# Sixty-four chunks of tokens stand in the array and the state weights stream: a new injection for the bidirectional scan, with its states in token order

## The chip, the cores and the metric

The kernel runs on one core of one Trainium2 chip. The metric is the device time of one execution in microseconds (us); lower is better. Changes of under 0.2% can't be told from no change here.

## The reference, cut to what matters

Four layers of a diffusion backbone, batch 1, 256 latent tokens and 256 context tokens, width 1024, float32. Every layer is a token mixer and a SwiGLU channel mixer; each half ends in a join (residual, RMS norm, shift and scale from modulation vectors that come from `silu(c) @ mod_w + mod_b`, four layers times six vectors of 1024). The mixers are latent attention, Hyena, S5 and FNet, in this order. The change is in layer 2, the S5 mixer:

```python
# S5_GROUPS = 64 groups of 16 channels, S5_STATE = 64 complex states, two directions
def s5_scan(u, lam_bar, b_bar, h0, reverse):
    bu = jnp.einsum('bngc,gsc->bngs', u.astype(jnp.complex64), b_bar)
    a = jnp.broadcast_to(lam_bar, bu.shape)
    a_cum, xs = lax.associative_scan(_lin_rec, (a, bu), axis=1, reverse=reverse)
    ...
    return xs + a_cum * h0[:, None]      # x[t] = lam_bar * x[t-1] + b_bar u[t]
...
xs_ctx = s5_scan(u_ctx, ..., None, reverse)          # context first
xs_lat = s5_scan(u_lat, ..., h0, reverse)            # then the latents, from the context's last state
y_lat = y_lat + einsum(xs_lat, c_mat).real           # both directions are added
return a * jax.nn.sigmoid(b)   # a, b from gelu(y_lat) @ w_glu + b_glu
```

## The kernel before

Each engine runs its own list of instructions in program order, and semaphores tie the lists. The stages follow each other: setup, then for every layer mixer, join (`mid`), channel mixer (`Ffn`), join (`post`). Every matrix product but those of the S5 and FNet mixers and a few small ones is made of three products of rounded halves (lines 956 to 958).

**The S5 mixer** treats the sequence in chunks of STEP = 8 tokens, so that 256 latents are CH = 32 chunks and context and latents together are 64. Its weights are prepared during the channel mixers of layers 0 and 1 and wait in DRAM: `et` (what a chunk adds to the states), `m0` (what a chunk's tokens do to its own outputs), `f` (what the state before a chunk does to its outputs), and a table of powers.

1. The join before it writes the normed tokens into `h_split` (line 693), and 32 DMAs, 16 from SP's queue and 16 from GpSimd's (`tokens`, line 2253), bring them into `u`: for each of the 64 groups 128 partitions (8 tokens times 16 channels) and 64 chunks, latents first.
2. Injection (line 2475), in 16 rounds of four groups, NB = 16. The weights `et` stand in the array (128 columns, real and imaginary part apart) and the 64 chunks of `u` stream. A product of float32 shows as two passes in the trace, so 128 products are 256 passes. Partitions of the result are the states, 64 forward and 64 backward.
3. ScalarE takes each round's bank into `e` (line 2521) with three copies: context before latents for the forward direction, and reversed for the backward one. `e` holds for each group and part the place q in a block of 8 chunks first and the block b last, so a copy writes with a step of 32 bytes.
4. The scan runs on VectorE: `inside` (lines 2375 to 2378) goes from place to place for all 8 blocks at once, seven steps of four instructions, for groups 0 to 15, 16 to 31 and 32 to 63; `across` (2385 to 2388) goes from block to block on the last places, seven steps of four, for the first half (groups 0 to 31) and for the second; `carries` (2430 to 2433) adds to the other places what comes in from the block before, eight instructions of 896 elements. `carries` of the first half is on GpSimd, that of the second on VectorE.
5. TensorE meanwhile makes the products with `m0` (line 2489), and after ScalarE and VectorE have brought the states into `s2` (line 2521, 2451, 2452) those with `f` (line 2502), first half and second half. The results are turned (2513), go through GELU, and the gated projection follows (line 864).

**The modulation vectors.** `mod_w` comes in 96 panels of 1 MB, two at a time in `mod_ring`. A planner (`mods.place`) puts each panel's product (line 397) at a fixed spot of TensorE's list; four panels make a vector. ScalarE then moves its rows (line 408) when its own list comes there, TensorE turns them (line 374), and VectorE adds the bias (line 418). `place` also puts the turn of a finished vector at the next spot, whether that spot has panels of its own or none, and gives the point of SP's list where the slot is filled again (line 360). A join has two spots, part 0 before the spread of `r_post` and part 1 after that of `r_pre`. Before, the join ahead of S5 has two panels in each part; S5 has 2 in `states`, 4 in `scan` and 2 in `turns`; the later joins have two in part 0, and the last one before FNet an empty part 1 that turns the last vector, ahead of FNet's first product. The join after FNet has none.

The spaces `t0`, `t1`, `raw` and `tab` lie in the ring of weight panels; `lab` (bank 3) and `scaled` (bank 2) are in PSUM. GpSimd doesn't read PSUM here.

## Time and profile before

| what | value |
|---|---|
| median of 3 runs | 2223.07 us (2221.59 to 2223.78) |
| the profiled execution | 2222.09 us, of which the span is 2220.3 us |
| TensorE, matmuls | 2089.5 us busy, 94% of the span |
| VectorE | 1163.3 us, 52% |
| ScalarE | 865.4 us, 39% |
| GpSimd | 157.9 us, 7% |
| granted TensorE clock, mean | 0.965 of full |
| chain that ended last | TensorE 87%, VectorE 7%, ScalarE 2%, DMA 2% |
| the mixer, first injection to first product of the gated projection | 1547.1 to 1655.3 us |

A share of busy time is a mean over stages; a TensorE that is busy at the lower clock, or that mostly loads weights, shows as busy as one at its peak. So the stage is read by itself: its engines one after the other, and the chain through it.

### The profile page before, as it was taken

Reading aid. Unit: us, or ns where it says so; the run is one execution under the profiler, and the core shown is the slowest. Engines: PE = TensorE matmul, PEld = TensorE weight load, DVE = VectorE, ACT = ScalarE, POOL = GpSimd, SP = SyncE. Lnnn points to the kernel's source line nnn. Section 1 sums busy time; section 2 is a strip of 40 time slices with the busy share of each in tenths; the row PEclk is TensorE's granted clock in tenths of the full one; section 3 lists DMA queues with packets and bytes.
Section 4 is the critical chain, followed back from the end, with each engine's and each line's share of the span. In section 5 each row is a group of like instructions: output and inputs, shape, how many; then the busy total and the mean of one; then the engine's idle time right before and its main releaser. Section 6 shows DMA issues by size and latency. Waiting matters only on the chain.

```text
span 2220.3 us, 31627 instructions
## 1 busy us (share of the span) xinstructions
PE 2089.5 (94%) x13233; PEld 1641.6 (74%) x13233; DVE 1163.3 (52%) x1961; ACT 865.4 (39%) x1416; POOL 157.9 (7%) x225
## 2 busy tenths in 40 slices
PE   4999999999999989999999999997959999898998
PEld 2756567777777767766468878875947899788997
DVE  2332552655666566647164665755661645526454
ACT  2442334433333453231253333344632544515444
POOL 0000110102101100010010210111200000000000
PEclk8999999999999999999999999998579999999999
DMA  6335341545535546442153443444584555314553
GB/s 258 133 111 183 133 152 42 197 147 172 178 119 187 180 172 216 165 135 103 57 170 106 130 136 100 141 134 162 233 305 145 190 189 175 123 58 153 189 184 102
DMA packets 227243, 342.14 MB, mean 154 GB/s; under 512 B 9590, under 2 KB 190625, under 8 KB 224860
## 3 DMA queue, kind: packets, MB, share of 16 engines
q1 hardware_dynamic: 216064, 310.27, 40.8%
q0 software_dynamic: 10320, 29.58, 4.6%
q8 instruction: 105, 1.72, 0.3%
q10 hardware_dynamic: 716, 0.26, 0.0%
q14 instruction: 38, 0.31, 0.0%
HBM read 317.66 MB, written 24.51 MB: 154 GB/s over the span
## 4 chain that ended last, share of the span: by engine, by line
PE 87%; DVE 7%; ACT 2%; DMA 2%; issue 1%; SPq 0%; POOL 0%; ACTq 0%; DVEq 0%
PE bank L956 21%; PE bank L957 20%; PE bank L958 20%; PE bank L819 4%; PE bank L397 3%; PE bank L864 3%; PE bank L2475 2%; PE bank L1724 1%; PE bank L1351 1%; PE bank L637 1%; DMA arena<-mod_w 1%; PE bank L2057 1%; PE bank L627 1%; PE bank L495 1%; DVE arena L710 1%; DVE arena L721 1%
## 5 line engine op out<-in xcount | busy, mean ns | idle before, releaser
L956 PE MATMUL bank<-h_hi,w_hi 128*128 128x512 f32 (+1 forms) x1480 | 512.0, 346 | 11.8 <-DVE h_lo L725 11.2
L957 PE MATMUL bank<-h_lo,w_hi 128*128 128x512 f32 (+1 forms) x1480 | 504.4, 341 | 0.0
L958 PE MATMUL bank<-h_hi,w_lo 128*128 128x512 f32 (+1 forms) x1480 | 504.4, 341 | 0.0
L917 DVE TENSOR_TENSOR w_lo<-ring,w_hi 128x1024 fp32r<-128x1024 f32 (+1 forms) x282 | 323.8, 1185 | 284.6 <-ACT w_hi L910 284.5
L956 PEld LDWEIGHTS bank<-h_hi,w_hi 128*128 128x128 f32 x1480 | 283.0, 191 | 50.8 <-DVE h_lo L725 15.3
L910 ACT ACTIVATE w_hi<-ring 128x1024 fp32r<-128x1024 f32 (+1 forms) x282 | 274.0, 1019 | 102.0 <-PE bank L958 100.2
L958 PEld LDWEIGHTS bank<-h_hi,w_lo 128*128 128x128 f32 x1480 | 283.0, 191 | 32.0 <-issue 0.2
L957 PEld LDWEIGHTS bank<-h_lo,w_hi 128*128 128x128 f32 x1480 | 283.3, 191 | 29.2 <-issue 0.2
L956 PE MATMUL bank<-g_hi,w_hi 128*128 128x512 f32 (+1 forms) x704 | 241.1, 342 | 0.0
L957 PE MATMUL bank<-g_lo,w_hi 128*128 128x512 f32 (+1 forms) x704 | 236.9, 337 | 0.0
L958 PE MATMUL bank<-g_hi,w_lo 128*128 128x512 f32 (+1 forms) x704 | 236.7, 336 | 0.0
L956 PEld LDWEIGHTS bank<-g_hi,w_hi 128*128 128x128 f32 x704 | 133.5, 190 | 22.7 <-issue 8.7
L958 PEld LDWEIGHTS bank<-g_hi,w_lo 128*128 128x128 f32 x704 | 133.5, 190 | 14.3
L957 PEld LDWEIGHTS bank<-g_lo,w_hi 128*128 128x128 f32 x704 | 133.6, 190 | 12.9
L1076 ACT ACTIVATE g_hi<-arena 128x512 fp32r<-128x512 f32 (+1 forms) x88 | 45.9, 525 | 234.4 <-DVE arena L1101 234.4
L1070 ACT ACTIVATE arena<-bank 128x512 f32<-128x512 f32 (+1 forms) x88 | 42.8, 491 | 190.3 <-PE bank L958 188.6
L397 PE MATMUL bank<-mod_ring,silu_c 128*32 128x256 f32 x1408 | 94.1, 392 | 24.2 <-DMA mod_ring<-mod_w 24.1
L1101 DVE TENSOR_TENSOR arena<-arena,bank 128x512 f32<-128x512 f32 (+1 forms) x88 | 48.2, 551 | 112.4 <-PE bank L958 110.5
L397 PEld LDWEIGHTS bank<-mod_ring,silu_c 128*32 128x32 f32 x1408 | 39.5, 111 | 63.7 <-DMA mod_ring<-mod_w 29.2
L956 PE MATMUL bank<-h_hi,hy_w_hi 128*128 128x512 f32 x192 | 76.4, 398 | 0.8 <-DVE h_lo L725 0.7
L957 PE MATMUL bank<-h_lo,hy_w_hi 128*128 128x512 f32 x192 | 74.9, 390 | 0.0
L958 PE MATMUL bank<-h_hi,hy_w_lo 128*128 128x512 f32 x192 | 74.8, 390 | 0.0
(328 smaller groups left out, 2959.7 us busy)
## 6 DMA issues: line engine op xcount, KB each, us to landing
ring<-ffn_w SPq DMA_DIRECT2D x120, 1024.0 KB, 5.1
mod_ring<-mod_w SPq DMA_DIRECT2D x88, 1024.0 KB, 6.8
ring<-ffn_w SPq DMA_DIRECT2D x16, 768.0 KB, 4.6
ring<-hy_w_in SPq DMA_DIRECT2D x12, 1024.0 KB, 5.3
arena<-mod_w SPq DMA_DIRECT2D x8, 1024.0 KB, 17.3
s_in_weights<-arena POOLq DMA_DIRECT2D x32, 256.0 KB, 3.3
s_out_weights<-arena POOLq DMA_DIRECT2D x16, 512.0 KB, 3.4
arena<-s_in_weights SPq DMA_DIRECT2D x8, 1024.0 KB, 10.9
```

Source lines behind the costliest of these rows:

```text
L397: last = nc.tensor.matmul(MODB[32 * g:32 * g + 32, 0:256], silu_c[:, k, :], self.slot(m)[:, kk, 256 * g:256 * g + 256], start=(k == 0), st ...
L819: last = nc.tensor.matmul(self.banks[c % 4][:, 0:self.n], v[:, kl, q * P:(q + 1) * P], self.rhs(k), start=(k == 0), stop=(k == self.kk - 1))
L864: last = nc.tensor.matmul(self.bank(c, t)[:, 0:self.n], v[:, k, q * P:(q + 1) * P], self.rhs(k), start=(k == 0), stop=(k == KD - 1))
L910: nc.scalar.activation(self.hi[:, i % SPLIT, a:b], self.w.slot(i)[:, a:b], ACT.Copy).then_inc(w_rounded, 1)
L917: last = unit.tensor_tensor(self.lo[:, i % SPLIT, c:c + w], self.w.slot(i)[:, c:c + w], self.hi[:, i % SPLIT, c:c + w].bitcast(F32), ALU.s ...
L956: nc.tensor.matmul(o, w[0], v[0], start=first, stop=False)
L957: nc.tensor.matmul(o, w[0], v[1], start=False, stop=False)
L958: return nc.tensor.matmul(o, w[1], v[0], start=False, stop=last)
L1070: nc.scalar.activation(self.silus[:, q, 0:n], self.out(i, q)[:, 0:n], ACT.Silu).then_inc(ffn_silu, 1)
L1076: nc.scalar.activation(g_hi[:, c + q, 0:n], self.silus[:, q, 0:n], ACT.Copy).then_inc(ffn_g_rounded, 1)
L1101: nc.vector.tensor_tensor(self.silus[:, q, 0:n], self.silus[:, q, 0:n], self.out(i, q)[:, 0:n], ALU.mult).then_inc(ffn_product, 1)
L2475: last = nc.tensor.matmul(bank[self.INJECT[n % 2]][:, o:o + 2 * CH], self.et[:, c % 4, 4 * (n % 2) + gb, i, :], self.u[:, 4 * n + gb, :], ...
```

## The change

The mixer is another one, the products and sums are the same.

- **Standing tokens.** In a round the 64 chunks of a group's `u` stand (64 columns), and its `et` streams with 256 columns. Two groups share the array, with outputs in partitions 0 to 63 and 64 to 127. A round is 4 products of 256 columns in place of 8 of 64. The result has chunks on partitions, so it is copied whole to `rows` (in `t0`), by VectorE in rounds 0 to 3 and by ScalarE in the others (`move_injected`), and four transposes on TensorE turn it into bank 4 or 5 (`turn_states`). ScalarE then makes two copies of 64x512 into `e`, one plain and one reversed.
- **Order of tokens.** The join puts the context at place 0 of `h_split` and the latents at 1. `e` has the block first and the place in it last, so that chunks lie in the tokens' order: ScalarE's copies in and out are of neighbouring elements, and `forward` and `backward` are one copy each. In `inside`, a place's blocks now lie 32 bytes apart.
- **GpSimd.** It runs `across` for the first half as well, before its `carries`, with the factors copied to SBUF (`signed`), and waits for all 32 copies into `e` first, since its scratch is `rows`.
- **Modulations.** The join before S5 keeps two panels in part 0 and none after; `states` has 4, `scan` 2, `turns` 2. The joins after it have no part 1 at all, and the join after FNet gets the last two panels in its part 0.
- SP's queue: the two refills ahead of `tokens` are gone; the later four loads of `et` stand ahead of the other refills and of the loads of `m0`.

```diff
@@ -567,7 +567,7 @@
 def place_mods(self, counts=(2, 2), before=None):
-    self.fills = True
+    self.fills = len(counts)
     for part, n in enumerate(counts):
         mods.place((self, part), n, len(panels) + 2 if before is None else before[part])
...
@@ -650,7 +650,7 @@
     if self.pre:
         pe.wait_ge(*self.small.after(7 if self.post else 2))
         spread(bank[4], r_pre, self.n).then_inc(j_spread, 1)
-    if self.fills:
+    if self.fills == 2:
         mods.tensor(pe, (self, 1))
...
+                dst = h_split[:, :, k, 1 - a // LAT, :].rearrange("p s m -> p m s")
             last = nc.scalar.activation(dst, src, ACT.Identity, bias=mod.shift(f > 1, k, s), scale=mod.factor(f, k, s))
         last.then_inc(h_shifted, 1)
...
                 self.first.round(act, 2, 0)
     if self.fills:
-        for part in range(2):
+        for part in range(self.fills):
             mods.scalar(act, (self, part))
...
 PARTS = ((slice(0, 16), slice(16, 32)), (slice(32, 64),))
-SCAN = [4 * (BLK - 1) * n + 4 * (2 * CH // BLK - 1) + c for n, c in ((2, 0), (1, 8))]
+ACROSS, CARRIES = 4 * (2 * CH // BLK - 1), 8
+SCAN = [4 * (BLK - 1) * 2, 4 * (BLK - 1) + ACROSS + CARRIES]
...
@@ -2257,6 +2260,7 @@
     self.ffn.finished(pool)
     for qt in range(4):
         self.tokens(pool, 1, qt)
+    pool.wait_ge(self.e_moved, 2 * self.NB)
     pool.wait_ge(self.step, self.SCAN[0])
     steps = [0]
@@ -2265,12 +2269,14 @@
         ins.then_inc(self.carried, 1)
         if wait:
             pool.wait_ge(self.carried, steps[0])
-    self.carries(nc.gpsimd, slice(0, 32), self.t0, self.raw.rearrange("p i s g -> p (i s g)"), then)
+    gs = slice(0, 32)
+    self.across(nc.gpsimd, gs, self.t0[:, 0:64], self.t0[:, 64:128], (self.signed[:, 0], self.signed[:, 1]), then)
+    self.carries(nc.gpsimd, gs, self.t0, self.raw.rearrange("p i s g -> p (i s g)"), then)
...
-    self.e = area(4096, GROUPS, 2, STEP, 2 * CH // BLK)
...
+    self.signed = spare[:, 2048 + 896:2048 + 1024].rearrange("p (a g r) -> p a g r", a=2, r=2)
+    self.rows = self.t0.rearrange("p (a n) -> p a n", a=2)
...
     p0 = len(panels)
-    mods.place((self, "turn"), 0)
-    mods.place((self, "states"), 2, p0 + 0.3)
-    mods.place((self, "scan"), 4, p0 + 0.4)
+    mods.place((self, "states"), 4, p0 + 0.4)
+    mods.place((self, "scan"), 2, p0 + 0.4)
     mods.place((self, "turns"), 2, p0 + RING)
...
@@ -2320,18 +2327,17 @@
     for c in range(4):
         inject(c)
     sp.dma_start(self.raw.rearrange("p i s g -> p (i s g)"), s5w.tab_dram).then_inc(self.m_loaded, 16)
-    mods.refill(sp, p0 + 0.1)
     for qt in range(4):
         self.tokens(sp, 0, qt)
+    for c in range(4, 8):
+        inject(c)
     mods.refill(sp, p0 + 0.2)
     sp.wait_ge(s5w.m_stored, 16 * STEP * 4)
     sp.wait_ge(self.m_loaded, 16)
     for c in range(8):
         toeplitz(c)
-    for c in range(4, 8):
-        inject(c)
-    sp.wait_ge(self.e_summed, self.NB)
+    sp.wait_ge(self.e_summed, self.injected(self.NB - 1))
     for hf in range(2):
         if hf:
...
+    for n in range(2):
+        self.move_injected(dve, V.tensor_copy, n)
...
-    dve.wait_ge(self.placed, 16)
+    dve.wait_ge(self.placed, 2 + 16)
+    for a in range(2):
+        V.tensor_copy(self.signed[:, a], self.lab[:, 2 + a, 0:32]).then_inc(self.placed, 1)
+    for n in range(2, 4):
+        self.move_injected(dve, V.tensor_copy, n)
...
         for i in range(1, BLK):
-            prev, cur = self.e[:, gs, :, i - 1, :], self.e[:, gs, :, i, :]
+            prev, cur = self.e[:, gs, :, :, i - 1], self.e[:, gs, :, :, i]
             scan(V.tensor_tensor(ta, wide(0), prev, ALU.mult), False)
             scan(V.tensor_tensor(tb[:, :, ::-1, :], wide(1), prev, ALU.mult))
             scan(V.tensor_tensor(ta, ta, tb, ALU.add))
             scan(V.tensor_tensor(cur, cur, ta, ALU.add))
...
     for hf in range(2):
         for gs in self.PARTS[hf]:
-            dve.wait_ge(self.e_moved, 3 * gs.stop // 4)
+            dve.wait_ge(self.e_moved, 2 * gs.stop // 4)
             inside(gs)
-            if gs.start == 0:
-                mods.vector(dve, (self, "turn"))
-        across(slice(32 * hf, 32 * hf + 32))
-    dve.wait_ge(self.carried, 8)
+    gs = slice(32, 64)
+    self.across(V, gs, self.scaled[:, 0:64], self.t1[:, 0:64], (self.lab[:, 2, gs], self.lab[:, 3, gs]), scan)
+    dve.wait_ge(self.carried, self.ACROSS + self.CARRIES)
     self.carries(V, slice(32, 64), self.t0, self.t1, scan)
...
+def across(self, unit, gs, ta, tb, factors, scan):
+    ends = self.e[:, gs, :, :, BLK - 1]
+    ta, tb = (v.rearrange("p (g r) -> p g r", r=2) for v in (ta, tb))
+    for b in range(1, 2 * CH // BLK):
+        prev, cur = ends[:, :, :, b - 1], ends[:, :, :, b]
+        scan(unit.tensor_tensor(ta, factors[0], prev, ALU.mult), False)
+        scan(unit.tensor_tensor(tb[:, :, ::-1], factors[1], prev, ALU.mult))
+        scan(unit.tensor_tensor(ta, ta, tb, ALU.add))
+        scan(unit.tensor_tensor(cur, cur, ta, ALU.add))
...
-    tq = [self.tab[:, i, 0:nq, gs].rearrange("p q g -> p g q").unsqueeze(3).to_broadcast([P, n, nq, 4]) for i in range(2)]
-    end = [self.e[:, gs, r, nq, 3:7].unsqueeze(2).to_broadcast([P, n, nq, 4]) for r in range(2)]
-    u0, u1 = (v[:, 0:n * nq * 4].rearrange("p (g q b) -> p g q b", q=nq, b=4) for v in (t0, t1))
+    tq = [self.tab[:, i, 0:nq, gs].rearrange("p q g -> p g q").unsqueeze(2).to_broadcast([P, n, 4, nq]) for i in range(2)]
+    end = [self.e[:, gs, r, 3:7, nq].unsqueeze(3).to_broadcast([P, n, 4, nq]) for r in range(2)]
+    u0, u1 = (v[:, 0:n * nq * 4].rearrange("p (g b q) -> p g b q", q=nq, b=4) for v in (t0, t1))
     for r, (x0, x1, op) in enumerate(((0, 1, ALU.subtract), (1, 0, ALU.add))):
-        cur = self.e[:, gs, r, 0:nq, 4:8]
+        cur = self.e[:, gs, r, 4:8, 0:nq]
...
 def states(self, rows, hf):
     gs = slice(32 * hf, 32 * hf + 32)
-    dst = self.s2[rows, gs].rearrange("p g r (i m) -> p (g r) i m", m=BLK)
-    src = self.e[rows, gs].rearrange("p g r q b -> p (g r) b q")
-    return dst, src
+    return self.s2[rows, gs].rearrange("p g r m -> p (g r) m"), self.e[rows, gs].rearrange("p g r b q -> p (g r) (b q)")[:, :, CH - 1:2 * CH - 1]
 def forward(self, act, copy, hf, done):
     dst, src = self.states(slice(0, STATE), hf)
-    copy(dst[:, :, :, 0], src[:, :, 3:7, BLK - 1]).then_inc(done, 1)
-    copy(dst[:, :, :, 1:BLK], src[:, :, 4:8, 0:BLK - 1]).then_inc(done, 1)
+    copy(dst, src).then_inc(done, 1)
 def backward(self, eng, copy, hf, done):
     dst, src = self.states(slice(STATE, P), hf)
-    copy(dst[:, :, ::-1, BLK - 1], src[:, :, 3:7, BLK - 1]).then_inc(done, 1)
-    copy(dst[:, :, ::-1, BLK - 2::-1], src[:, :, 4:8, 0:BLK - 1]).then_inc(done, 1)
-INJECT, OUT, TURNED = (0, 1), (0, 1, 4, 5), ((0, 1), (4, 5))
+    copy(dst[:, :, ::-1], src).then_inc(done, 1)
...
+def injected(self, n):
+    return 2 * n if n else 1
+def turned(self, n):
+    return min(2 * n + 3, 2 * self.NB)
+def moved(self, n):
+    return n + 1 + (18 if n >= 2 else 0)
+def inject(self, pe, n):
+    c = n // 2
+    if n % 4 == 0:
+        for e in range(2):
+            pe.wait_ge(self.u_loaded[e][n // 4 % 2], 16 * 4 * (n // 8 + 1))
+    if n % 2 == 0:
+        pe.wait_ge(self.w_loaded[c % 4], 16 * (c // 4 + 1))
+    if n >= 2:
+        pe.wait_ge(self.placed, self.moved(n - 2))
+    for p in range(2):
+        for z in range(2):
+            gb = 2 * p + z
+            last = nc.tensor.matmul(bank[self.INJECT[n % 2]][64 * z:64 * z + 64, 256 * p:256 * p + 256], self.u[:, 4 * n + gb, :],
+                                    self.et[:, c % 4, 4 * (n % 2) + gb].rearrange("p i n -> p (i n)"), start=True, stop=True)
+    last.then_inc(self.e_summed, 1)
...
+def move_injected(self, eng, copy, n):
+    eng.wait_ge(self.e_summed, self.injected(n))
+    if n >= 2:
+        eng.wait_ge(self.e_summed, self.turned(n - 2))
+    copy(self.rows[:, n % 2], bank[self.INJECT[n % 2]][:, :]).then_inc(self.placed, 1)
+def turn_states(self, pe, n):
+    pe.wait_ge(self.placed, self.moved(n))
+    if n >= 2:
+        pe.wait_ge(self.e_moved, 2 * (n - 1))
+    dst = bank[self.STATES[n % 2]][:, :].rearrange("p (a z i j) -> p a i z j", a=2, z=2, i=2)
+    for p in range(2):
+        for i in range(2):
+            o = 256 * p + P * i
+            last = nc.tensor.transpose(dst[:, p, i], self.rows[:, n % 2, o:o + P], ident[:, :])
+    last.then_inc(self.e_summed, 1)
...
+    for n in range(self.NB + 1):
+        if n < self.NB:
+            self.inject(pe, n)
+        if n:
+            self.turn_states(pe, n - 1)
...
-    for idx in (*range(8, 16), *range(8)):
+    for idx in range(16):
         hf, gl = divmod(idx, 8)
-        if idx == 0:
-            pe.wait_ge(self.e_moved, 3 * self.NB)
+        if idx == 8:
+            pe.wait_ge(self.e_moved, 2 * self.NB)
         for j in range(4):
-            last = nc.tensor.matmul(out(idx, j), self.u[:, self.place(hf, gl, j), 0:CH], self.m0[:, 8 * (4 * hf + j) + gl, :],
+            last = nc.tensor.matmul(out(idx, j), self.u[:, self.place(hf, gl, j), CH:2 * CH], self.m0[:, 8 * (4 * hf + j) + gl, :],
...
-        pe.wait_ge(self.s_moved, 4 if hf == 0 else 6)
+        pe.wait_ge(self.s_moved, 2 if hf == 0 else 3)
         if hf:
-            pe.wait_ge(self.moved_dve, 2)
+            pe.wait_ge(self.moved_dve, 1)
...
     for n in range(self.NB):
-        act.wait_ge(self.e_summed, n + 1)
-        src = bank[self.INJECT[n % 2]][:, :].rearrange("p (g b q) -> p g b q", g=8, q=BLK)
-        dst = self.e[:, 4 * n:4 * n + 4].rearrange("p g r q b -> p (g r) b q")
-        copy(dst[0:STATE, :, 4:8], src[0:STATE, :, 0:4]).then_inc(self.e_moved, 1)
-        copy(dst[0:STATE, :, 0:4], src[0:STATE, :, 4:8]).then_inc(self.e_moved, 1)
-        copy(dst[STATE:P, :, ::-1, ::-1], src[STATE:P]).then_inc(self.e_moved, 1)
-    act.wait_ge(self.carried, 8)
+        if n == 3:
+            act.wait_ge(self.placed, self.moved(3))
+        if 3 <= n < self.NB - 1:
+            self.move_injected(act, copy, n + 1)
+        act.wait_ge(self.e_summed, self.turned(n))
+        src = bank[self.STATES[n % 2]][:, :].rearrange("p (a m) -> p a m", m=CH)
+        dst = self.e[:, 4 * n:4 * n + 4].rearrange("p g r (a b) q -> p (g r a) (b q)", a=2)
+        copy(dst[0:STATE], src[0:STATE]).then_inc(self.e_moved, 1)
+        copy(dst[STATE:P, :, ::-1], src[STATE:P]).then_inc(self.e_moved, 1)
+    mods.scalar(act, (self, "states"))
+    act.wait_ge(self.carried, self.ACROSS + self.CARRIES)
     self.forward(act, copy, 0, self.s_moved)
     self.backward(act, copy, 0, self.s_moved)
-    for key in ("turn", "states", "scan"):
-        mods.scalar(act, (self, key))
+    mods.scalar(act, (self, "scan"))
     act.wait_ge(self.step, sum(self.SCAN))
     self.forward(act, copy, 1, self.s_moved)
...
@@ -2645,15 +2688,15 @@
 mixer = MIXER[l](pre, mid, n_in, n_out, ffn)
 if l < 2:
     mid.place_mods()
-if l == 2:
-    mid.place_mods((2, 0))
+else:
+    mid.place_mods((2,))
 ffn = Ffn(l, n_out, mid, post, TICKS[l])
 if l == 0:
     post.place_mods()
 if l == 1:
-    post.place_mods((2, 2), (len(panels) + 0.1, len(panels) + 0.2))
+    post.place_mods((2, 0), (len(panels) + 0.2, None))
 if l == 2:
-    post.place_mods((2, 0))
+    post.place_mods((2,))
 stages += [mixer, mid, ffn, post]
 post2 = post
```

## Rows read from the trace of the kernel before

**Rows 1.** Stretches of 4 us: busy PE, PEld, DVE, ACT, POOL; clock; DMA share; GB/s.
```profile
1532.00:1536.00 4.00, 0.00 (x0) 0.00 (x0) 4.00 (x8) 3.14 (x5) 0.06 (x1) 0.68 0.99 412
...
1596.00:1600.00 4.00, 4.00 (x21) 4.00 (x20) 0.13 (x1) 2.83 (x5) 3.78 (x2) 0.50 0.00 0
...
1624.00:1628.00 4.00, 3.46 (x96) 3.19 (x88) 3.58 (x17) 0.00 (x0) 0.00 (x0) 0.80 1.02 413
```

**Rows 2.** The chain that ended last, through the mixer: start us, us, what.
```profile
1547.08 27.57 PE bank L2475 x128
...
1640.20 3.82 ACT tail L2521 x2
1644.11 6.30 PE bank L2502 x128
...
1655.43 27.63 PE bank L864 x128
```

**Rows 3.** Timeline of VectorE: start us, us, instruction, idle before it and its releaser.
```profile
1563.39 0.43 DVE L2375 TENSOR_TENSOR bank<-bank,arena 128x256 f32<-128x256 f32 x1 [16.97 <-ACT arena L2521]
...
1574.91 0.42 DVE L2378 TENSOR_TENSOR arena<-arena,bank 128x256 f32<-128x256 f32 x1
...
1604.69 0.70 DVE L2375 TENSOR_TENSOR bank<-bank,arena 128x512 f32<-128x512 f32 x1 [8.56 <-ACT arena L2521]
...
1624.12 0.27 DVE L2385 TENSOR_TENSOR bank<-bank,arena 128x64 f32<-128x64 f32 x1
...
1631.43 1.09 DVE L2430 TENSOR_TENSOR ring<-ring,arena 128x896 f32<-128x896 f32 x1
```

**Rows 4.** The same view of GpSimd and ScalarE.
```profile
1596.22 2.32 POOL L2430 TENSOR_TENSOR ring<-ring,arena 128x896 f32<-128x896 f32 x1 [46.24 <-DVE arena L2388]
...
1614.22 7.69 ACT L2521 ACTIVATE tail<-arena 64x256 f32<-64x256 f32 x4 [9.63 <-POOL arena L2433]
```

**Rows 5.** The same view of TensorE, at half and at full clock.
```profile
1544.87 1.94 PE L397 MATMUL bank<-mod_ring,silu_c 128*32 128x256 f32 x16 [3.69 <-DMA mod_ring<-mod_w]
...
1628.48 1.07 PE L397 MATMUL bank<-mod_ring,silu_c 128*32 128x256 f32 x16 [1.02 <-DMA mod_ring<-mod_w]
...
1650.34 1.09 PE L2513 MATMUL bank<-ident,arena 128*128 128x128 f32 x8
```

**Rows 6.** Groups by line and shape: busy us, mean ns, idle before, releasers.
```profile
L2521 ACT ACTIVATE arena<-bank 64x256 f32<-64x256 f32 x32 | 18.0, 667 | 21.1 <-PE bank L2475 21.1
L1442 ACT ACTIVATE arena<-bank 64x512 f32<-64x512 f32 x8 | 4.7, 591 | 26.8 <-PE bank L958 26.8
...
L2385 DVE TENSOR_TENSOR bank<-bank,arena 128x64 f32<-128x64 f32 x14 | 3.7, 266 | 0.5
L2387 DVE TENSOR_TENSOR bank<-bank,ring 128x64 f32<-128x64 f32 x14 | 3.3, 232 | 0.5
L2452 DVE COPY tail<-arena 64x1792 f32<-64x1792 f32 x1 | 1.8, 1773 | 0.0
...
L917 POOL TENSOR_TENSOR mla_o_lo<-ring,mla_o_hi 128x256 fp32r<-128x256 f32 x16 | 11.8, 771 | 247.2 <-ACT mla_o_hi L910 247.2
```

**Rows 7.** Two lines of the S5 weights' preparation: ns min/median/max, first and last start us.
```profile
L2128 DVE TENSOR_TENSOR arena<-arena x64: 681/908/1150, 504.8 to 1475.1; 128x512 f32<-128x512 f32 x64
L2129 DVE TENSOR_TENSOR arena<-arena x64: 681/686/703, 505.8 to 1475.7; 128x512 f32<-128x512 f32 x64
```

**Rows 8.** Timeline of the join before FNet and of FNet's start.
```profile
1935.76 0.60 ACT L693 ACTIVATE h_sb<-arena,modv,affine 128x256 f32<-128x256 f32 x1 [0.34 <-DVE arena L721]
...
1942.46 0.69 PE L374 MATMUL bank<-ident,mod_rows 128*128 128x128 f32 x2 [8.19 <-ACT mod_rows L408]
1942.95 8.81 PE L2595 MATMUL bank<-arena,h_sb 128*128 128x256 f32 x32
...
1944.90 0.69 DVE L2614 COPY arena<-bank 128x512 f32<-128x512 f32 x1 [1.32 <-PE bank L2595]
```

**Rows 9.** Timeline of VectorE in the join after FNet.
```profile
2002.92 1.21 DVE L917 TENSOR_TENSOR w_lo<-ring,w_hi 128x1024 fp32r<-128x1024 f32 x1
```

More of the change, by code:

```diff
@@ L550, in __init__ @@
                 self.rows = n // 4
-                self.first, self.fills = None, False
+                self.first, self.fills = None, 0
                 self.sq = Tally(y_squared, KD)
@@ L776, in vector @@
                 if self.fills:
-                    for part in range(2):
+                    for part in range(self.fills):
                         mods.vector(dve, (self, part))
@@ L2378, in inside @@
                         scan(V.tensor_tensor(cur, cur, ta, ALU.add))
-                def across(gs):
-                    ends = self.e[:, gs, :, BLK - 1, :]
-                    ta, tb = (v[:, 0:(gs.stop - gs.start) * 2].rearrange("p (g r) -> p g r", r=2) for v in (self.scaled, self.t1))
-                    for b in range(1, blocks):
-                        prev, cur = ends[:, :, :, b - 1], ends[:, :, :, b]
-                        scan(V.tensor_tensor(ta, self.lab[:, 2, gs], prev, ALU.mult), False)
-                        scan(V.tensor_tensor(tb[:, :, ::-1], self.lab[:, 3, gs], prev, ALU.mult))
-                        scan(V.tensor_tensor(ta, ta, tb, ALU.add))
-                        scan(V.tensor_tensor(cur, cur, ta, ALU.add))
                 for hf in range(2):
                     for gs in self.PARTS[hf]:
-                        dve.wait_ge(self.e_moved, 3 * gs.stop // 4)
+                        dve.wait_ge(self.e_moved, 2 * gs.stop // 4)
                         inside(gs)
-                        if gs.start == 0:
-                            mods.vector(dve, (self, "turn"))
-                    across(slice(32 * hf, 32 * hf + 32))
-                dve.wait_ge(self.carried, 8)
+                gs = slice(32, 64)
+                self.across(V, gs, self.scaled[:, 0:64], self.t1[:, 0:64], (self.lab[:, 2, gs], self.lab[:, 3, gs]), scan)
+                dve.wait_ge(self.carried, self.ACROSS + self.CARRIES)
                 self.carries(V, slice(32, 64), self.t0, self.t1, scan)
```

28 lines of the change are left out of this document (6 added, 22 removed).

## The prediction

> **What bounds the kernel now.** I read the page's shares first, and they don't help here: TensorE is busy for 94% of the span, but the change touches a stage in which it is busy at the wrong thing. Then the chain of waits through the mixer [rows 2]: 55 us of injection without a gap, a second part in which VectorE and ScalarE end the waits, the products with the second half's states from 1644.11. So two questions set the stage: how early the scan gets its states, and how long the scan and what hangs on it take. The clock view answers the first: it falls to 0.50 when TensorE waits for the join, and is still 0.50 at 1596 with TensorE full [rows 1]. 128 columns stand and only 64 stream, 256 passes in 55.1 us or 0.215 us a pass; this is paid whatever VectorE does. The timelines answer the second [rows 3]: VectorE starts at 1563.39, does two parts of `inside`, `across`, then waits 8.56 us for the last states, and goes from 1604.69 to 1640.20 without a gap. GpSimd's `carries` (1596.22 to 1614.22, [rows 4]) is beside all this.
>
> **The change part by part.**
>
> *Injection.* A round is 4 products (8 passes) of 256 columns, two at a time in the array. Passes of 256 columns with four sharing the array take 1.94 / 16 = 0.121 us each at half clock and 1.07 / 16 = 0.067 at full [rows 5]; with two sharing I double this: 1.94 or 1.07 us for the 8. Four transposes cost 4 x 1.09 / 8 = 0.54 us at full clock [rows 5], some 0.85 at half. TensorE so needs 2.8 us a round at half clock and 1.6 at full, against 3.44 now. ScalarE needs a copy of 128x512 and two of 64x512: 3 x 0.59 by the 64x512 row [rows 6] is 1.8 us; if the reversed one costs what its stepped copies do now (667 ns for 256, so about 1.1 for 512), 2.3. The slower of the two sets the pace, 1.8 to 2.8 us.
>
> *Start of the scan.* The refills' 2 MB no longer go ahead of the tokens, for which injection waited; but VectorE is in the join until 1544.1 anyway and then makes the first two copies (0.6 us each) and the powers' placement (3 us), and the copies of rounds 2 and 3. Round 3's states are in `e` at 1552 to 1555.5, full or half clock; I take 1553.5, 9.9 us before now. The 16th round is in at 1571 (ScalarE's pace) to 1587 (half clock to the end).
>
> *VectorE, `inside`.* Four instructions take (1575.33 - 1563.39) / 7 = 1.71 us for 16 groups and (1624.12 - 1604.69) / 7 = 2.78 for 32 [rows 3]. Now blocks lie 32 bytes apart. Line 2128 is the same product with neighbouring or 32-byte-stepped output: 0.681 against 1.150 us for 512 elements, while line 2129, never stepped, stays at 0.69 [rows 7]. One instruction in four writes stepped: +0.46 for 512, +0.24 for 256. Two more only read stepped. A copy that reads stepped shows nothing (1792 elements in 1.77 us), `across` shows (266 - 232) ns for 64 elements at a step of 256 bytes, 0.5 ns an element [rows 6]. I take half of that: +0.14 and +0.28 a step. So 14 x 2.09 = 29.3 us and 7 x 3.52 = 24.6, where before it was 24.0 and 19.4: 10 us lost, and 7.3 of `across` no longer in the way. Unhurt it would be 43.4 in all; with reads as dear as writes 14 x 2.42 + 7 x 4.16 = 63.0. First half done at 1553.5 + 29.3 = 1582.8, about when even the slow injection is done; `inside` of the second half at 1607.4, its `across` (7.31 us, [rows 3]) at 1614.7.
>
> The Trainium skill, SBUF — State Buffer, "Door 1: The DMA port swizzle", says that accesses which cross to a new 16-byte line each time pay, reads and writes alike. The stepped write agrees with it; the stepped copy doesn't, as it reads at the full rate. By the rule the sum for VectorE would be nearer 63 us, by the rows 54.
>
> *GpSimd, `across`.* The trace has no product of 64 elements there. 0.77 us for 256 and 2.32 for 896 [rows 4, 6] give 2.4 ns an element or, with the cheaper 2.08 of the same group, 2.05; I take 0.38 us and 0.07 between dependent ones: 28 x 0.45 = 12.6 us. Bounds: VectorE's own 7.3 (it was never faster than that), and the 256-element price each time, 28 x 0.84 = 23.5. `carries` took 18.0; its table is now read at 256 bytes' step, for which I add 1.5 (0 to 3.5). So 1582.8 + 12.6 + 19.5 = 1614.9, level with VectorE, whose own `carries` (8.8 us from 1631.43 to 1640.20, [rows 2, 3], plus 1) end at 1624.7. What GpSimd delays is late twice: VectorE's `carries` and ScalarE's copies both wait for it.
>
> *From there to the last product with `f`.* ScalarE's copies of the first half took 7.69 us [rows 4], most of it at a 32-byte step; two plain ones of 2048 elements cost 2 x 1.8 by the 64x512 price, I take 4.3 as one is reversed: 1619.2. TensorE: 5.4 us of products (half of it at half clock) and two panels, 2.1 to 3.9 by [rows 5]: 1627.2. On ScalarE the move of a finished vector stands ahead of `forward` of the second half and waits for those panels: 0.4, then 1.9 for the copy and 0.3 of handing over: the second half's products start at 1629.8 instead of 1644.11. **-14.3 us.** VectorE's `backward`, done at 1627, is not the last. DMA: loads of `et` for rounds 8 and up go out at 1548, four rounds ahead; `m0` and `f` (12 MB at the 0.41 MB/us of [rows 1], 30 us) and two panels are in by 1608, and the gated projection's weights are asked for at 1628, 13 us before use as now. `states` with its four panels waits for two of them, until about 1608, under the wait for 1619. Cover: 11 us.
>
> *Joins.* The join before FNet no longer turns a vector after itself. Now TensorE stands 8.19 us for ScalarE's move of it, ahead of FNet's first product at 1942.95, though the first normed tokens are ready from 1936.4 [rows 8]. VectorE can take the first of the eight banks at 1941.5, after the join, not at 1944.90; by then four of FNet's eight sets of products (0.86 us each at full clock, 1.7 at half) are done or nearly; the last four follow at about one in 0.9: they end at 1945.8 instead of 1951.75. **-5.9 us**, 3 if TensorE stays at half clock. The join after FNet gets two panels (1.9 us) ahead of the spread; VectorE is on line 917 until 2004.12 [rows 9], which hides them but for 0.1. The turn that moves from the join after S5 to the one before FNet cancels out; the last vector is turned inside the last channel mixer, 0.4 us of TensorE, taken in full.
>
> **Sum**, against the profiled execution (2222.09, span 2220.3): -14.3 - 5.9 + 0.4 = -19.8, so 2202.3. The median lies 1.0 above the profiled one: **2203.3 us**.
>
> **The rivals.**
> - *GpSimd's short instructions cost nearly as much as long ones.* For it: `across` has 28 dependent little instructions, and the smallest product on GpSimd here is 0.77 us. Then its part ends 11 us later (23.5), the second half's products start at 1640.7, total -8.9: **2214**. From 0.45 us each on, every 0.1 us costs 2.8 us.
> - *Half clock and stepped reads at the price of writes.* Scan begins at 1555.5, the first half is done at 1589.4, GpSimd ends at 1623 to 1625 and the products start at 1639: -5, and FNet -3: **2215**. For it: the clock stayed at 0.50 through 55 us of busy TensorE; against it: it rose inside the products with `f` [rows 1].
> - *Steps are nearly free and GpSimd is quick.* `inside` as now, `across` 7.3, `carries` 18.0: GpSimd ends at 1603, the products start at 1617: -27, total -33: **2190**. Against it: line 2128. With only the reads free and GpSimd at 0.35, 2198.
> - *The other side: two products of 64 standing columns don't share the array.* The trace shows sharing for 32 columns only. At half clock a round would then be 8 x 0.485 + 0.85 = 4.7 us, the states complete at 1620 instead of 1602, GpSimd at 1652 and the products at 1667: +23 - 5.9, **2240**. It decides from about 3.9 us a round. Against it: four groups share perfectly (0.067 us a pass against 27.63 / 128 = 0.216 for the same columns alone, [rows 2, 5]), and at full clock even unshared it is 2.3 a round.
>
> **Chances.** Forecast (2199 to 2208) 0.5; GpSimd dear 0.15; half clock with dear reads 0.13; steps free or nearly 0.15; unshared 0.03; the rest, a wait that I don't see, 0.04, half of it at no change. Range for 8 in 10: 2192 to 2216. Faster by over 0.2% (4.4 us, about what can be told from no change): all but the last two and a little of the dear ones, 0.92; within 0.04; slower 0.04.
>
> **What would show it.** After: line 2475's successor in 16 rounds of 1.8 to 2.8 us; first `inside` near 1553.5, 2.09 us a step, its writing instruction at 0.66; GpSimd's 28 little products with their mean (0.38 expected) and its end near 1615; VectorE's wait for it of about 0; ScalarE's copies of the first half 4.3 us; products with `f` of the second half near 1630; FNet's first product 6 us after the join's spread instead of 9. The prediction is wrong where GpSimd's short products or the stepped reads are priced wrong, or where the pace of injection is above 2.8 us.

## The result, and the profile after

The changed kernel takes **2206.16 us** (median of 4 runs, 2204.82 to 2207.84); the kernel before took 2222.74 in the 4 runs beside it (2221.59 to 2223.78). The ratio is 0.9926, 95% interval 0.9909 to 0.9943, a gain of 16.6 us. The profiled execution took 2206.80 us, with a span of 2205.0 against 2220.3. The same points of the two profiles, from their timelines:

| point | before | after | difference |
|---|---|---|---|
| join before S5, first spread (L495) | 1527.39 | 1528.32 | +0.9 |
| first instruction of `inside` | 1563.39 | 1553.82 | -9.6 |
| second half's products with `f` | 1644.11 | 1634.34 | -9.8 |
| gated projection | 1655.27 | 1644.65 | -10.6 |
| join before FNet, first spread | 1931.49 | 1922.10 | -9.4 |
| FNet's token products | 1951.59 | 1936.33 | -15.3 |
| end of the span | 2220.3 | 2205.0 | -15.3 |

The two kernels are the same ahead of the first point; its +0.9 is not of the change. In later profiles here that point lies anywhere from 1527.4 to 1529.5, so one profile places a stage to about 1 us, and intervals inside it are worth more than its absolute times.

The injection first. Windows of the changed kernel (us, busy PE, PEld, DVE, ACT, POOL, clock, DMA share, GB/s), to read beside [rows 1]:

```profile
1532.00:1544.00 12.00, 2.43 (x12) 1.55 (x13) 11.32 (x20) 8.52 (x12) 4.19 (x8) 0.50 0.68 201
...
1548.00:1572.00 24.00, 22.22 (x166) 12.50 (x164) 20.05 (x44) 21.97 (x40) 1.81 (x4) 1.00 0.98 370
1592.00:1608.00 16.00, 3.87 (x32) 1.19 (x32) 15.55 (x18) 0.00 (x0) 14.94 (x18) 0.50 0.88 344
```

The clock is at its lower level (0.50 is 1.2 GHz of 2.4) in the two windows in which TensorE mostly waits, and at full speed from 1548 to 1572, with 256 columns streaming a pass; before, with 64, it was at 0.50 through the injection. No run here isolates what made the difference. TensorE's timeline, with the successor of [rows 2, 5]:

```profile
1542.42 3.29 PE L2492 MATMUL bank<-arena 128*64 128x256 f32 x16 [9.57 <-DMA arena<-h_sb]
...
1546.92 1.08 PE L2492 MATMUL bank<-arena 128*64 128x256 f32 x8
1547.94 0.66 PE L2511 MATMUL bank<-ident,ring 128*128 128x128 f32 x4
...
1601.61 1.94 PE L397 MATMUL bank<-mod_ring,silu_c 128*32 128x256 f32 x16 [14.25 <-DMA mod_ring<-mod_w]
...
1619.08 5.93 PE L2542 MATMUL bank<-arena,tail 128*32 128x128 f32 x128 [13.10 <-ACT tail L2561]
1624.82 1.91 PE L397 MATMUL bank<-mod_ring,silu_c 128*32 128x256 f32 x32
1634.34 5.14 PE L2542 MATMUL bank<-arena,tail 128*32 128x128 f32 x128 [7.61 <-ACT tail L2561]
```

Eight passes take 1.08 us at full clock (0.135 a pass) and the transposes 0.66; two products share the array. Later rounds follow each other every 1.72 us, which is ScalarE's three copies. Panels wait for DMA until 1601.6, under cover as forecast. Now VectorE, the view of [rows 3]:

```profile
1553.82 0.63 DVE L2387 TENSOR_TENSOR bank<-bank,arena 128x256 f32<-128x256 f32 x1 [3.11 <-ACT arena L2561]
1554.35 0.61 DVE L2388 TENSOR_TENSOR ring<-bank,arena 128x256 f32<-128x256 f32 x1
1555.00 0.43 DVE L2389 TENSOR_TENSOR bank<-bank,ring 128x256 f32<-128x256 f32 x1
1555.46 0.63 DVE L2390 TENSOR_TENSOR arena<-arena,bank 128x256 f32<-128x256 f32 x1
1556.13 0.62 DVE L2387 TENSOR_TENSOR bank<-bank,arena 128x256 f32<-128x256 f32 x1
...
1586.08 1.08 DVE L2387 TENSOR_TENSOR bank<-bank,arena 128x512 f32<-128x512 f32 x1
...
1632.26 1.23 DVE L2458 COPY tail<-arena 64x2048 f32<-64x2048 f32 x1
```

A step of four is 2.31 us where it was 1.71. Of the four only L2389 touches nothing stepped, and it alone keeps its 0.43. The groups by line and shape (busy us, mean ns) say the same of the long form and of the other engines' parts:

```profile
L2390 DVE TENSOR_TENSOR arena<-arena,bank 128x512 f32<-128x512 f32 x7 | 7.6, 1092 | 0.2
L2387 DVE TENSOR_TENSOR bank<-bank,arena 128x512 f32<-128x512 f32 x7 | 7.6, 1086 | 0.2
...
L2389 DVE TENSOR_TENSOR bank<-bank,ring 128x512 f32<-128x512 f32 x7 | 4.9, 699 | 0.2
L2442 DVE TENSOR_TENSOR ring<-ring,arena 128x896 f32<-128x896 f32 x2 | 3.4, 1711 | 0.1
```

```profile
L2442 POOL TENSOR_TENSOR ring<-ring,arena 128x896 f32<-128x896 f32 x2 | 4.7, 2339 | 0.2
...
L2429 POOL TENSOR_TENSOR ring<-ring,arena 128x64 f32<-128x64 f32 x7 | 2.4, 350 | 36.9 <-DVE arena L2390 36.4
```

`inside` lasts 60.0 us in all (1553.82 to 1613.79), `across` of the second half 7.2, and VectorE's carries 11.2 (1621.02 to 1632.26), as two of their four products read the table at a step of 256 bytes (1.71 us instead of 1.09). GpSimd is done at 1614.93, so VectorE doesn't wait for it. ScalarE's timeline, the successor of [rows 4]:

```profile
1614.96 3.97 ACT L2561 ACTIVATE tail<-arena 64x2048 f32<-64x2048 f32 x2 [28.09 <-POOL arena L2445]
1626.79 0.38 ACT L408 ACTIVATE mod_rows<-bank 128x256 f32<-128x256 f32 x1 [7.86 <-PE bank L397]
1632.26 1.98 ACT L2561 ACTIVATE tail<-arena 64x2048 f32<-64x2048 f32 x1 [5.08 <-DVE arena L2445]
```

The last row is the reading of the whole stage: ScalarE stood 5.08 us ready, and VectorE's last carry released it. From there back to the start of `inside` the chain is VectorE's alone; nothing of GpSimd's or of the first half's products is on it. And FNet's start, to read beside [rows 8]:

```profile
1924.17 0.71 PE L495 MATMUL bank<-r_pre,sel 64*128 64x128 f32 x4 [1.37 <-DVE r_pre L759]
1926.18 0.67 PE L2638 MATMUL bank<-arena,h_sb 128*128 128x256 f32 x2 [1.30 <-ACT h_sb L694]
...
1936.33 13.98 PE L2647 MATMUL bank<-arena 128*128 128x256 f32 x64
```

### The profile page after: what moved, and what is told of

The parts are those of the page before. It is cut to its first block, busy times and chain, and to the rows that moved or that the text cites. A ratio compares the mean times of both kernels' runs of the same rounds, so it can differ in the third digit from the quotient of the medians.

```text
span 2205.0 us, 31525 instructions
## 1 busy us (share of the span) xinstructions
PE 2065.0 (94%) x13169; PEld 1605.4 (73%) x13169; DVE 1177.0 (53%) x1938; ACT 848.8 (38%) x1409; POOL 167.1 (8%) x253
## 4 chain that ended last, share of the span: by engine, by line
PE 86%; DVE 8%; DMA 3%; ACT 2%; issue 1%; SPq 0%; POOL 0%; ACTq 0%; DVEq 0%
PE bank L957 21%; PE bank L958 20%; PE bank L959 20%; PE bank L820 4%; PE bank L397 4%; PE bank L865 3%; PE bank L1725 1%; PE bank L1352 1%; DMA mod_ring<-mod_w 1%; PE bank L637 1%; DMA arena<-mod_w 1%; PE bank L2058 1%; PE bank L627 1%; DVE arena L2390 1%; DVE bank L2387 1%; PE bank L1936 1%
## 5 line engine op out<-in xcount | busy, mean ns | idle before, releaser
L957 PEld LDWEIGHTS bank<-h_hi,w_hi 128*128 128x128 f32 x1480 | 284.0, 192 | 47.3 <-DVE h_lo L726 11.2
L959 PEld LDWEIGHTS bank<-g_hi,w_lo 128*128 128x128 f32 x704 | 133.5, 190 | 14.3
L617 DVE TENSOR_TENSOR tail<-x_sb,arena 128x512 f32<-128x512 f32 (+1 forms) x48 | 26.6, 554 | 90.8 <-ACT arena L595 86.1
```

The source lines that it names most:

```text
L617: nc.vector.tensor_tensor(self.zx[:, c % 2, 0:n // P, 1, :], x[:, c, 0:n].rearrange("p (g t) -> p g t", t=P), Y[:, c, 0:n].rearrange("p (g ...
L957: nc.tensor.matmul(o, w[0], v[0], start=first, stop=False)
L959: return nc.tensor.matmul(o, w[1], v[0], start=False, stop=last)
```

## The experiments

**Theory 1**: the new injection starts the scan early; then VectorE alone sets the second half, with instructions lengthened by reads 32 bytes apart as well as writes; FNet's part is separate and additive. **Rivals**: GpSimd or the first half ends last; VectorE's instructions are long because of a neighbour on the same memory; FNet's gain depends on the mixer. The runs of the first three sections stand beside the kernel before at 2222.74 us. Those of "More work on GpSimd" and "Forward first" were taken at another time and stand beside it at 2222.08, so a difference from one group to the other can be off by 0.7 us.

### FNet's part alone

```diff
# kernel before
-mods.place((self, "scan"), 4, p0 + 0.4)
+mods.place((self, "scan"), 2, p0 + 0.4)
-if l == 2: mid.place_mods((2, 0))
+if l >= 2: mid.place_mods((2,))
-if l == 2: post.place_mods((2, 0))
+if l == 2: post.place_mods((2,))
```

> The kernel before, with its mixer untouched; only the places of the modulation panels after the mixer are those of the changed kernel: the mixer's 'scan' gets 2 panels in place of 4, the joins before the last feed-forward, before FNet and after FNet get two each in part 0, and no part 1 turns a vector ahead of FNet's first product. Theory 1 (the steps add up, and FNet's part is -5.9 and the last turn +0.4): 5.5 us faster than before, FNet's first product about 1.3 us after the join's second spread instead of 9, its eight channel products over 5.9 us sooner behind that spread. Rival (the profile's 5.9 depends on when the mixer ends, and the two panels ahead of the last join's spread are paid): 2 to 4 us faster.

Measured: 2216.69 us against 2222.74, ratio 0.9975 (0.9965 to 0.9985): 6.0 us faster, with an interval of 3.3 to 7.8. Its profile:

```profile
1935.25 0.71 PE L495 MATMUL bank<-r_post,sel 64*128 64x128 f32 x4
...
1939.33 0.67 PE L2595 MATMUL bank<-arena,h_sb 128*128 128x256 f32 x2 [1.30 <-ACT h_sb L693]
...
1949.48 13.98 PE L2604 MATMUL bank<-arena 128*128 128x256 f32 x64
```

From the first spread to the token products it is 14.23 us, where the kernel before has 20.10 and the changed one 14.23: 5.87 less, to the hundredth. Theory 1 holds for this interval, and by the medians the mixer's own share of the 16.6 is about 10.6. The profile as a whole shows less: counted from the join before S5 (1529.29 here) the FNet join begins 1.9 later than in the kernel before, most of it in two panels at the lower clock (3.32 us for 1.86), and the end comes 4.5 sooner.

### Place first in memory again

```diff
# changed kernel
-self.e = area(4096, GROUPS, 2, 2 * CH // BLK, BLK)
+self.e = area(4096, GROUPS, 2, BLK, 2 * CH // BLK)
-dst = bank[...].rearrange("p (a z i j) -> p a i z j", a=2, z=2, i=2)          # turn_states
+dst = bank[...].rearrange("p (a z i q j) -> p a i z j q", a=2, z=2, i=2, q=BLK)
-    copy(dst[STATE:P, :, ::-1], src[STATE:P]).then_inc(self.e_moved, 1)
+    for a in range(2):
+        copy(dst[STATE:P, :, ::-1, a, ::-1], src[STATE:P, :, :, a]).then_inc(self.e_moved, 1)
# inside, across, carries, states, forward, backward index e and s2 as in the kernel before
```

> The changed kernel with the memory order of `e` before (place first, block last), while chunks keep the tokens' order in `h_split`; TensorE's transposes write PSUM in that order, so ScalarE's forward copy stays one run and the backward one becomes two copies of 64x256; the copies out of `e` are the four stepped ones of before. Theory 1 (VectorE's instructions are long because they read 32 bytes apart, and VectorE alone sets the second half): `inside` takes 24.0 + 19.4 = 43.4 us instead of 60.0, the carries 8.8 instead of 11.2; GpSimd starts at about 1578 and ends at 1607, VectorE follows at 1615, ScalarE's copies out cost 7.7 + 3.8, the products with f of the second half start at 1622 to 1625 instead of 1634.3, some 10 us faster than the changed kernel, near 2196. Rival 2 (not the step makes them long but a neighbour at work on the same memory, ScalarE's copies above all): `inside` stays near 60, the copies out cost 5.6 more, and the kernel is 2 us slower than the changed one.

Measured: 2199.57 us (2197.92 to 2200.01), 6.6 faster than the changed kernel. Groups of VectorE, and ScalarE's timeline:

```profile
L2387 DVE TENSOR_TENSOR bank<-bank,arena 128x256 f32<-128x256 f32 x14 | 6.0, 432 | 3.7 <-ACT arena L2567 3.2
L2390 DVE TENSOR_TENSOR arena<-arena,bank 128x256 f32<-128x256 f32 x14 | 5.9, 421 | 0.5
...
L2387 DVE TENSOR_TENSOR bank<-bank,arena 128x512 f32<-128x512 f32 x7 | 4.9, 699 | 0.2
...
L2442 DVE TENSOR_TENSOR ring<-ring,arena 128x896 f32<-128x896 f32 x2 | 2.2, 1094 | 2.5 <-POOL arena L2445 2.5
```

```profile
1605.89 7.75 ACT L2567 ACTIVATE tail<-arena 64x256 f32<-64x256 f32 x4 [18.91 <-POOL arena L2445]
1621.33 0.38 ACT L408 ACTIVATE mod_rows<-bank 128x256 f32<-128x256 f32 x1 [7.69 <-PE bank L397]
1621.74 3.81 ACT L2567 ACTIVATE tail<-arena 64x256 f32<-64x256 f32 x2
```

With the same neighbours at work VectorE's instructions are short again (432 ns for 624, 699 for 1086): the step made them long, and the contention rival falls. `inside` of the first half ended at 1576.8 after 24.0 us. TensorE wrote PSUM in the new order at no price (0.66 us for the four transposes as before), and a round took 1.77 us against 1.72. But the products with `f` came only at 1625.65, not 1622 to 1625: `forward` was ready to go at 1614.7 and ran at 1621.74, behind the move of a modulation vector (L408) that waits for panels behind the first half's products. That is 7 us of a wait that had been hidden.

### The table of powers, and across given back

```diff
# changed kernel, one kernel each
-self.raw, self.tab = (... .rearrange("p (i s g) -> p i s g", i=2, s=BLK) for i in range(2))
+self.tab = spare[:, 3072:4096].rearrange("p (i g s) -> p i s g", i=2, s=BLK)     # neighbouring q
```

> The changed kernel with the table of powers laid out with the place q last, so that VectorE's carries of the second half read neighbouring words. Theory 1: the four products of the carries fall from 1.67-1.75 us to 1.1, 2.4 us in all, and as VectorE alone sets the second half all of it is in the total: 2203.8. Rival (GpSimd's or ScalarE's part of the first half, or a DMA, ends last): 0. Placing the table may write stepped, at most 0.5 us, ahead of the scan, where VectorE waits 3.1 us anyway.

```diff
-self.across(nc.gpsimd, slice(0, 32), ..., then)
+for hf in range(2):      # after inside of each half
+    self.across(V, slice(32 * hf, 32 * hf + 32), ..., scan)
```

> The changed kernel with `across` of the first half given back to VectorE; GpSimd does only its carries. Theory 1 (VectorE alone sets the second half, GpSimd has 5 to 6 us to spare): 7.2 us slower than the changed kernel, 2213.4. Rival (GpSimd's end is what sets it, VectorE's time is hidden): GpSimd ends 4 us sooner, and the kernel gets faster by up to 4.

The table: 2204.02 us (2203.08 to 2204.29), 2.1 faster, and VectorE's products fall from 1711 to 1092 ns. GpSimd reads the same table, and its products fall too, from 2339 ns:

```profile
L2443 POOL TENSOR_TENSOR ring<-ring,arena 128x896 f32<-128x896 f32 x2 | 3.8, 1916 | 0.2
```

So the step of 256 bytes costs GpSimd 0.42 us on 896 elements, and GpSimd ends 1.8 sooner here. `across` on VectorE: 2212.74 us (2211.63 to 2213.76), 6.6 slower, although GpSimd then ended at 1610.6, 4.3 sooner. Two terms of opposite sign on VectorE come out at nearly their own size in the total. The table alone doesn't tell VectorE from GpSimd, as both got faster; `across` does, since there GpSimd got faster and the kernel slower.

### More work on GpSimd

```diff
+for i in range(2):       # between across and carries
+    then(nc.gpsimd.tensor_tensor(extra, extra, extra, ALU.mult))     # extra: 128x896 of its scratch
```

> The changed kernel with two more products of 896 elements on GpSimd between its `across` and its carries (extra work on its scratch, no result of it is used): 4.6 us more. Theory 1 (VectorE alone sets the second half; GpSimd has 6.1 us before VectorE's carries, and ScalarE and TensorE 5.1 us before `forward`): no change, 2206.2, and VectorE's carries still start at 1621.0. Rival (GpSimd's end sets it too): +4.6, 2210.8.

Measured: 2206.26 us (2205.04 to 2207.08), no change. The dose was smaller than planned, 3.44 us, since both inputs are the same tile:

```profile
1596.74 3.44 POOL L2276 TENSOR_TENSOR ring<-ring 128x896 f32<-128x896 f32 x2
```

ScalarE's copies of the first half moved from 1614.96 to 1618.04, and the products with `f` of the second half stayed (1634.08). `forward` of the second half still waited for VectorE, for 1.76 us. GpSimd is off the path of the changed kernel with at least 3 us to spare.

### Forward first, and three more ways

```diff
# place-first kernel
-mods.scalar(act, (self, "scan"))
 act.wait_ge(self.step, sum(self.SCAN))
 self.forward(act, copy, 1, self.s_moved)
+mods.scalar(act, (self, "scan"))
```

> The place-first kernel of the run before, with one step moved: on ScalarE `forward` of the second half now stands ahead of the move of the finished modulation vector, which waits for panels that TensorE makes only after the first half's products. There VectorE was done with the second half at 1614.7, ScalarE free at 1613.6, and `forward` started only at 1621.7 behind that move. Theory 1 (with the scan short, this order is what ends last): `forward` runs 1614.7 to 1618.6, the second half's products follow the two panels at 1621.3 instead of 1625.65, 4.4 us faster: 2195.2. Rival (the wait in front of the second half's products is for something else, a transfer of f or a bank): no change, 2199.6.

Measured: 2196.04 us (2194.96 to 2197.02), 3.5 faster than place-first and 10.1 than the changed kernel, or 2.9 and 9.5 if each is taken against the kernel before beside it. From the join before S5 to the gated projection the profiles differ by 3.8. The chain shows what took over:

```profile
1615.52 5.60 PE bank L2548 x128
1621.12 1.77 PE bank L397 x32
...
1623.37 10.45 DMA ring<-s_w_glu
...
1633.86 6.31 PE bank L865 x28
```

The products with `f` now follow the panels at once (1622.65), but the gated projection waits for its weights. Their DMA stands in SP's queue behind a refill of `mod_ring` that those same panels release. The forecast of -4.4 missed this: TensorE stands idle for 0.90 us there.

On top of it, the first half's `backward` on GpSimd (`self.backward(pool, nc.gpsimd.tensor_copy, 0, self.carried)` after its carries, and no longer on ScalarE):

> The kernel with `forward` first, and the first half's `backward` (two copies, 64x256 and 64x1792) made by GpSimd after its carries instead of by ScalarE. ScalarE's part of 7.75 us falls to 3.9. Theory 1: at GpSimd's 2.1 to 2.3 ns an element the copies take 4.2 to 4.8 us, the first half's products start 3.2 us sooner, and the second half's at about 1618.7, when `forward` is done: 2.6 us faster, 2192.6. Rival (GpSimd reads and writes these stepped words much more slowly, over 8 us): the same or slower.

Measured: 2195.01 us (2193.63 to 2195.90), 1.0 faster with overlapping ranges, not 2.6, and the mixer isn't faster at all: the second half's products come 80.87 us behind the first injection product, where it was 79.71, and the gated projection 0.5 later too. Timelines of GpSimd and VectorE:

```profile
1607.23 4.15 POOL L2465 COPY tail<-arena 64x1792 f32<-64x1792 f32 x1
```

```profile
1606.77 1.38 DVE L2443 TENSOR_TENSOR ring<-ring,arena 128x896 f32<-128x896 f32 x1 [2.54 <-POOL arena L2446]
1608.07 4.26 DVE L2444 TENSOR_TENSOR ring<-ring,arena 128x896 f32<-128x896 f32 x1
1612.37 1.09 DVE L2445 TENSOR_TENSOR ring<-ring 128x896 f32<-128x896 f32 x1
```

GpSimd's copy takes 4.15 us, as expected; but VectorE's product of 1.09 us takes 4.26, until 0.95 us after the copy's end at 1611.38, and VectorE is done 3.2 us late. Neither theory had this. The Trainium skill, SBUF — State Buffer, "Who interferes with whom", says that a VectorE instruction with two inputs in SBUF and a GpSimd one that reads SBUF exclude each other for their whole length; this row agrees. `inside` has one input in PSUM, and ran beside GpSimd's `across` and `carries` at its usual 699 ns.

And with `across` of the first half on VectorE:

> The kernel with `forward` first, with `across` of the first half on VectorE instead of GpSimd. Theory 1: VectorE's chain gets 7.3 longer and no longer waits 2.5 for GpSimd, so it ends at 1619.6 instead of 1614.8 and `forward` at 1623.5; GpSimd ends at 1602, and the second half's products start at 1623.6 instead of 1621.3: 2.3 us slower, 2197.5. So giving `across` to GpSimd would be worth 2.3 us with short instructions on VectorE, where it was worth 6.6 with long ones. Rival (the first half's end, 4 us sooner here, sets the time): faster by up to 4.

Measured: 2195.43 us (2195.25 to 2196.85), the same as with GpSimd's `across` (2196.04). The trace has the products with `f` 2.4 us later behind the first injection product (82.15 against 79.71 us), as expected, and the gated projection 2.6 later. By the join before the last channel mixer 1.6 of it had come back, in the two panels there, at the lower clock with GpSimd's `across` (first line) and at full clock without (second):

```profile
1697.67 3.69 PE L397 MATMUL bank<-mod_ring,silu_c 128*32 128x256 f32 x30
1698.97 2.08 PE L397 MATMUL bank<-mod_ring,silu_c 128*32 128x256 f32 x30
```

So with short instructions the part given to GpSimd is worth 2.4 us at the second half's products, and nothing of it was measured in the total; with long ones it was worth 6.6 in the total. The same 1.6 stands in the profile of the run with GpSimd's `backward`, which is 0.5 behind at the gated projection and 1.2 ahead at that join. Why the clock is lower in this join in some profiles stays open.

### How far apart is far

```diff
# place-first kernel, tb of inside only
+step = {0: 2, 16: 4, 32: 2}[gs.start]       # words between neighbours: 8, 16 and 8 bytes
+tb = self.t1[...].rearrange("p (g r b s) -> p g r b s", r=2, b=blocks, s=step)[:, :, :, :, 0]
```

> The place-first kernel with only the scratch tile `tb` of `inside` spaced out: its elements lie 8 bytes apart in the first 16 groups, 16 bytes apart in the second 16, and 8 bytes apart in the 32 of the second half. Everything else is contiguous, so the product that writes `tb` (0.41 us for 256 elements, 0.68 for 512 when contiguous) shows a step in the output alone, and the sum that reads it (0.43 and 0.70) shows it in one input alone. Theory 1 (an instruction pays once for a 16-byte line touched per element, whichever operand it is, 0.75 ns an element in the changed kernel at 32 bytes): at 16 bytes both cost the full +0.2 for 256 elements, at 8 bytes half of it, +0.1 for 256 and +0.2 for 512. Rival 1 (any step costs the same): +0.2 and +0.4 everywhere. Rival 2 (the price of a read comes from PSUM and SBUF operands together or from the width of the jump, only at 32 bytes and more): nothing at 8 and 16 bytes.

One execution, 2200.39 us; only the instructions' durations are read from it. VectorE's timeline in the first and in the second 16 groups, L2390 writing `tb`, L2391 reading it:

```profile
1557.90 0.41 DVE L2390 TENSOR_TENSOR ring<-bank,arena 128x256 f32<-128x256 f32 x1
1558.35 0.43 DVE L2391 TENSOR_TENSOR bank<-bank,ring 128x256 f32<-128x256 f32 x1
...
1571.06 0.60 DVE L2390 TENSOR_TENSOR ring<-bank,arena 128x256 f32<-128x256 f32 x1
1571.69 0.61 DVE L2391 TENSOR_TENSOR bank<-bank,ring 128x256 f32<-128x256 f32 x1
```

At 8 bytes neither pays (nor in the 512 form, 681 and 700 ns); at 16 bytes each pays +0.18 to +0.19, and at 32 bytes it was +0.19 for the same 256 elements. So theory 1 had the 16 bytes right and the 8 bytes wrong (it expected half), and both rivals fall. Steps between 8 and 16 bytes weren't tried. Read and write cost alike, and L2390 of the changed kernel, which does both, pays once. The Trainium skill, SBUF — State Buffer, "Specifications (TRN2)", asks for two hits on each line of 16 bytes for full speed; these four rows agree with it.

## Why the prediction was right, and where it wasn't

- **Injection.** Right in mechanism, and a little quicker than its range: 1.60 to 1.72 us a round (forecast 1.8 to 2.8), the array shared, the clock at full speed from 1546 on (0.70 in 1544 to 1546, 1.00 in 1546 to 1548), the reversed copy no dearer than the plain one (all 32 take 572 to 598 ns). First `inside` at 1553.82 (1553.5).
- **`inside`: the step that was mis-sized.** The prediction took stepped reads at half of 0.5 ns an element and got 53.9 us; measured 60.0, near its bound of 63.0. A stepped read costs as much as a stepped write, 0.75 ns an element: the two that only read take +0.38 a step together instead of the +0.14 put down (+0.78 instead of +0.28 in the long form), the one that writes +0.20 instead of +0.24. The reason given against it was wrongly read: the stepped copy of [rows 6], 1773 ns for 1792 elements, isn't at full rate. The plain copy in the changed kernel takes 1.23 us for 2048, 0.60 ns an element against 0.99. No plain copy of that size stood beside it, and the row was taken as free. Its price, 0.39 ns an element, is still about half of what the instructions with two inputs pay; no run here tells why.
- **The sum's path: wrong.** The prediction had VectorE and GpSimd level at 1615 and let the first half end last: GpSimd, ScalarE's copies, the first half's products, two panels, the move, then `forward`, with VectorE's carries done at 1624.7 and out of the way. That chain came out as forecast (GpSimd at 1614.93, the move done at 1627.17), but it wasn't last: VectorE's carries ended at 1632.26. It ended `across` at 1621.02 instead of 1614.7, and its carries took 11.2 instead of 9.8, since the far-stepped table costs them 2.4 us where 1 was put down. So the second half's products came at 1634.34 instead of 1629.8, and the forecast -14.3 became -9.8 (-10.7 counted from the join before S5).
- **GpSimd: right by luck.** Its end at 1614.93 is three misses that cancel: it started 3.4 later, `across` took 11.0 us instead of 12.6, carries 17.7 instead of 19.5. The +1.5 for the table was put on top of [rows 4], where the product of 2.32 us steps through the table by 256 bytes as well (each word four times over) and so probably holds that price already; with a table of neighbouring words it is 1.92.
- **Copies out.** 3.97 us for two (4.3), 1.98 for `forward` (1.9). DMA cover held: the panels' products were done at 1606, under a wait until 1619.
- **Behind them.** Those products ran at the higher clock more of the time (5.14 us for 6.30; clock 0.72 from 1634 to 1640, 0.54 from 1644 to 1650 before), and the panels in the next join at the lower one more of the time (2.98 us for 1.86, clock 0.63 against 1.00): -10.6 at the gated projection, -9.4 at FNet's join. The prediction had neither.
- **Joins.** FNet -5.87 (-5.9), shown alone by the first run. The join after FNet: no loss. The +0.4 for the last turn didn't show in the span.
- **The rivals.** GpSimd's short instructions aren't dear (0.35 us); the array was shared; steps are not free. Of "half clock and dear reads" only the reads came true. The reading of [rows 1] is a little off: 1532 to 1536 shows 0.68, and 0.50 comes in the stretch after.

The total landed 2.9 us above the forecast and inside its range: the parts add up as said, FNet's at its size and the mixer's short by what VectorE's stepped reads cost. Left open: the profiles wander by up to 1.6 us in the join before the last channel mixer with its clock (1.86 us for 32 passes, 3.34 for 30 of them), and nothing here controls it.

## What to carry to other kernels

Before a layout is changed so that one engine's copies get contiguous, count on every other engine the instructions that then touch only one word in each 16 bytes: here the copies out of `e` won 5.6 us on ScalarE, and `inside` and the carries lost 16.6 + 2.4 on VectorE, which ends last. A permutation may be free where TensorE writes it into PSUM on a transpose that is there anyway. Compare a price with a row of the same form that surely doesn't pay it; a row without such a neighbour shows no price even where it holds one. When the longest wait is cut, look in the engines' lists for the next small step that stands ahead of the released one; here it was a move of 0.38 us that held a copy for 7.
